# Feed-forward down projections on one core: pairs of chunks as seven block products, weight sums made by adding transfers

## The chip, the cores and the metric

The kernel runs on one NeuronCore of a Trainium2 chip. The metric is the device time of one execution in microseconds (us), as the median of several runs. Engines are named as the profile names them: PE (TensorE), DVE (VectorE), ACT (ScalarE), POOL (GpSimd), SP (SyncE, which here only issues transfers). 1 MiB is 1.0486 MB.

## What is computed

Two stacked model blocks on 256 tokens of width 1024. The first has two layers (a state-space mixer, then a neighbourhood attention), each with two feed-forward parts; these four are what the change is about, and the code numbers them 0 to 3:

```python
def swiglu(x, w_gu, w_down):                 # w_gu: 1024 x 5632, w_down: 2816 x 1024
    g, u = jnp.split(x @ w_gu, 2, axis=-1)
    return (jax.nn.silu(g) * u) @ w_down
...
h = h + 0.5 * swiglu(rmsnorm(h, ffn1_norm[i]), ffn1_w_gu[i], ffn1_w_down[i])
...
h = h + 0.5 * swiglu(rmsnorm(h, ffn2_norm[i]), ffn2_w_gu[i], ffn2_w_down[i])
gate = jax.nn.sigmoid(rmsnorm(h, ple_norm[i]) @ ple_w_gate[i])
```

The second block is an attention with three branches and a plain MLP. All is float32.

## The kernel before

**Precision.** PE multiplies in a reduced float32 form. So each operand is split into a high part and the rest (`whi` and `wlo` of a weight, `aThi` and `aTlo` of an activation), and each block product of 128 x 128 by 128 x 512 is three matmuls: high by high, high by low, low by high.

**Weight tiles.** `plan_of` (L156) lists all weight tiles in the order in which PE takes them. A tile is up to 2048 floats a partition, 1 MiB. SP's `load` (L498) brings it into one of four slots `raw`; it first waits until the split of the tile four places back is done. ACT copies it to `whi` (`ahead` in `scalar`, L1412) as soon as PE has released the tile three places back, DVE subtracts to get `wlo` (L1967), and PE's `take` waits for both. ACT, DVE and PE each run their own list in program order; `ahead` runs three tiles ahead of the work in it.

**A feed-forward part.** `ffn` goes over 11 column chunks c. A chunk takes two tiles `("up", i, c, 0)` and `(.., 1)`: 48 matmuls for both halves of the tokens. In the middle of chunk c PE turns the previous chunk's activation `fa` by four transposes (`turn_a`), ACT copies the bank to `aThi` (`high_a`) and DVE makes `aTlo` (`low_a`). At the end of a chunk ACT computes the silu and DVE the product (`fa`). Then `down` multiplies the 22 chunks of 128 rows of `w_down`: for each of the two column halves of 512, six tiles, for every 128-row chunk and each token half three matmuls, 264 in all. Banks 6 and 7 collect the left half, 2 and 3 the right one; DVE adds 0.5 times them to `h` (`residual`), and the turns of `h` for the next stage run within the right half.

**POOL** makes small statistics (`rstds`), some products of the mixer, and the bias tables `bm` of the neighbourhood attention from a table `tb`, which SP loads early in feed-forward part 2. No transfer is issued from POOL.

Of the kernel before, what the change touches and what calls it, by code (L numbers as in the profile page):

```python
# [12 lines left out]
P = 128  # L13
# [5 lines left out]
TILE = 2048  # L19

# [23 lines left out]
def constants():  # L44
# [30 lines left out]
    "a_weigh": "exps", "v_outputs": "yev yg yTlo", "a_outputs": "yThi ysq",  # L75
# [69 lines left out]
class Plan:  # L145
# [5 lines left out]
    def add(self, label, pieces, a, b):  # L151
        self.index[label] = len(self.tiles)
        self.tiles.append((pieces, a, b))


def plan_of(dr):  # L156
    p = Plan()

    def ffn(i, up, down, extra=None):
# [64 lines left out]
PREP = (8, 16, 24)  # L224
HALVES = 2 * len(PREP) + 2
# [129 lines left out]
def programs(dr, mem, banks, plan, ev):  # L355
# [11 lines left out]
    pool_tiles = set()  # L367
# [126 lines left out]
    def sync(S):  # L494
# [22 lines left out]
        def table():  # L517
            rp = dr["rpb"]
            S.wait_ge(*at("h", 4, 1, 1))
# [40 lines left out]
    def tensor(T):  # L560
# [13 lines left out]
        def take(*label):  # L574
# [5 lines left out]
            T.wait_ge(*at("w_lo_p" if n in pool_tiles else "w_lo", n))  # L580
# [115 lines left out]
        def closing_block(labels, bs, xhi, xlo, first, between=None):  # L696
# [6 lines left out]
            for t in range(2):  # L703
                for i, (label, hi, lo, kk) in enumerate(held):
                    nk = hi.shape[1]
                    for k in range(nk):
# [4 lines left out]
                        if between and t and i == 0 and k == 1:  # L711
                            between()
# [11 lines left out]
        def down(name, xhi, xlo, tiles, r, turn_last):  # L724

            for c in range(2):
                bs = ACC[c]
                clear(*bs)
                for y in range(tiles - 2):
# [3 lines left out]
                    if y == 0:  # L733
                        if c == 0:
                            turn_last()
                        elif r < 10:
                            turn(r, 0, 0)
                            turn(r, 1, 0)
                closing_block([name + (c, tiles - 2), name + (c, tiles - 1)], bs, xhi, xlo, 4 * (tiles - 2),
                              (lambda: turn(1, 0, 1)) if c and r == 1 else None)  # L740
                residual_in(r, c, bs)

        def ffn(i, r, extra=None):
# [24 lines left out]
            down(("down", i), aThi, aTlo, 6, r + 1, lambda: turn_a(10))  # L768
# [636 lines left out]
    def scalar(A):  # L1405
# [8 lines left out]
        def ahead(m):  # L1414
            while A.ready < min(m, len(plan.tiles)):
# [3 lines left out]
                if n >= NSPL:  # L1419
                    A.wait_ge(*at(*named(plan_labels[n - NSPL])))  # L1420
# [1392 lines left out]
```

## Time and profile before

| | |
|---|---|
| median of 3 runs | 1678.08 us (1678.04 to 1678.16) |
| profiled execution, span from first to last instruction | 1676.1 us |
| PE busy | 1664.8 us |
| DVE busy | 1068.0 us |
| ACT busy | 898.6 us |
| POOL busy | 86.1 us |
| DMA | 300.58 MB, 179 GB/s mean |

The page gives the profiled execution's span and no other time of its own; the median of the runs is 1.98 us longer than that span, which is what lies around the span. Busy time of PE overlaps from one matmul to the next, so a matmul's cost is read from the distance of two starts, not from its length. A DMA share is the time that packets took as a share of 16 engines; it can read above 1, because packets overlap.

### The profile page before, as it was taken

What the parts mean: (1) busy time and instruction counts of PE and PEld (TensorE: products, weight loads), DVE (VectorE), ACT (ScalarE), POOL (GpSimd) and SP (SyncE); (2) the same over time, 40 slices, a digit from 0 to 9 for tenths busy, and PEclk for the clock granted to TensorE, in tenths of its full rate; (3) what the DMA queues carried; (4) which work ended last, traced back from release to release, by engine and by line L of the source; (5) the groups of instructions that cost most, each with busy time, mean ns of one, the idle gap of its engine ahead of it and who ended that gap; (6) DMA issues with size and microseconds to landing.
All of it is one profiled execution on the core that took longest, in us unless ns stands there. A gap on an engine that the chain in (4) does not pass through costs nothing.

```text
span 1676.1 us, 23021 instructions
## 1 busy us (share of the span) xinstructions
PE 1664.8 (99%) x9366; PEld 1426.7 (85%) x9366; DVE 1068.0 (64%) x1364; ACT 898.6 (54%) x1279; POOL 86.1 (5%) x79
## 2 busy tenths in 40 slices
PE   8999999999999999999999999999999999999998
PEld 6888899999788888888888778888889999988886
DVE  5554678999965545755457766555655577766643
ACT  5443566777864444744346665444553556564532
POOL 0000000000100000000007500000000000000000
PEclk9999999999999999999999999999999999999999
DMA  9655567666466554686555336655565533465551
GB/s 306 192 178 184 158 191 208 179 196 209 156 200 198 187 188 165 188 242 209 181 175 195 119 101 214 185 180 188 180 197 153 174 103 126 152 211 178 176 192 60
DMA packets 243978, 300.58 MB, mean 179 GB/s; under 512 B 9248, under 2 KB 175520, under 8 KB 243872
## 3 DMA queue, kind: packets, MB, share of 16 engines
q1 hardware_dynamic: 238224, 289.25, 54.5%
q10 hardware_dynamic: 5648, 9.85, 2.2%
q8 instruction: 75, 1.23, 0.3%
q14 instruction: 31, 0.25, 0.0%
HBM read 297.96 MB, written 1.11 MB: 178 GB/s over the span
## 4 chain that ended last, share of the span: by engine, by line
PE 99%; DVE 1%; DMA 0%; ACT 0%; ACTq 0%; DVEq 0%; issue 0%
PE bank L564 95%; PE bank L567 4%; DMA h<-in_x 0%; DVE wlo L1967 0%; DVE hTlo L1970 0%; DVE xn L1970 0%; DVE h L1970 0%; ACT hThi L1412 0%; DVE xn L2019 0%; DVEq L2740 0%; ACT xn L1409 0%; ACTq L1924 0%; ACTq L1923 0%; ACT L1920 0%; ACTq L2740 0%
## 5 line engine op out<-in xcount | busy, mean ns | idle before, releaser
L1967 DVE TENSOR_TENSOR wlo<-raw,whi 128x2048 fp32r<-128x2048 f32 (+2 forms) x284 | 622.4, 2195 | 326.5 <-ACT whi L1412 326.5
L1412 ACT ACTIVATE whi<-raw 128x2048 fp32r<-128x2048 f32 (+2 forms) x284 | 518.2, 1832 | 244.8 <-PE bank L564 240.9
L564 PE MATMUL bank<-whi,hThi 128*128 128x512 f32 x1056 | 420.7, 398 | 0.0
L564 PE MATMUL bank<-wlo,hThi 128*128 128x512 f32 x1056 | 412.3, 390 | 0.3 <-DVE wlo L1967 0.3
L564 PE MATMUL bank<-whi,hTlo 128*128 128x512 f32 x1056 | 396.8, 391 | 0.0
L564 PE MATMUL bank<-hThi,whi 128*128 128x256 f32 x888 | 253.3, 285 | 0.0
L564 PE MATMUL bank<-hThi,wlo 128*128 128x256 f32 x888 | 251.2, 283 | 0.0
L564 PE MATMUL bank<-hTlo,whi 128*128 128x256 f32 x888 | 251.2, 283 | 0.0
L564 PEld LDWEIGHTS bank<-whi,hThi 128*128 128x128 f32 x1056 | 198.6, 188 | 44.3 <-issue 6.0
L564 PEld LDWEIGHTS bank<-whi,hTlo 128*128 128x128 f32 x1056 | 198.5, 188 | 42.6 <-DVE hTlo L1970 0.3
L564 PEld LDWEIGHTS bank<-wlo,hThi 128*128 128x128 f32 x1056 | 198.8, 188 | 40.5 <-DVE wlo L1967 1.8
L564 PEld LDWEIGHTS bank<-hThi,whi 128*128 128x128 f32 x888 | 169.5, 191 | 3.6 <-issue 3.1
L564 PEld LDWEIGHTS bank<-hThi,wlo 128*128 128x128 f32 x888 | 169.5, 191 | 0.2
L564 PEld LDWEIGHTS bank<-hTlo,whi 128*128 128x128 f32 x888 | 169.5, 191 | 0.2
L564 PE MATMUL bank<-whi,aThi 128*128 128x512 f32 x352 | 137.8, 391 | 0.0
L564 PE MATMUL bank<-whi,aTlo 128*128 128x512 f32 x352 | 137.1, 389 | 0.0
L564 PE MATMUL bank<-wlo,aThi 128*128 128x512 f32 x352 | 137.0, 389 | 0.0
L1412 ACT ACTIVATE aThi<-bank 128x512 fp32r<-128x512 f32 x44 | 26.3, 598 | 155.1 <-PE bank L567 155.1
L1409 ACT ACTIVATE ftmp<-bank,st 128x256 f32<-128x256 f32 x88 | 41.5, 475 | 105.6 <-PE bank L564 105.5
L2564 POOL TENSOR_TENSOR st<-st,cst 128x1 f32<-128x1 f32 (+2 forms) x35 | 36.5, 1057 | 1147.4 <-DVE st L1992 1075.2
L1967 DVE TENSOR_TENSOR aTlo<-bank,aThi 128x512 fp32r<-128x512 f32 x44 | 30.4, 691 | 80.8 <-ACT aThi L1412 80.8
L564 PEld LDWEIGHTS bank<-whi,aTlo 128*128 128x128 f32 x352 | 66.1, 188 | 13.8
(222 smaller groups left out, 1883.4 us busy)
## 6 DMA issues: line engine op xcount, KB each, us to landing
raw<-in_ffn_w_gu SPq DMA_DIRECT2D x172, 512.0 KB, 4.9
raw<-in_ffn_w_down SPq DMA_DIRECT2D x40, 1024.0 KB, 5.0
raw<-in_w_in SPq DMA_DIRECT2D x30, 1024.0 KB, 5.2
raw<-in_ssd_w_in SPq DMA_DIRECT2D x16, 1024.0 KB, 5.6
raw<-in_ssd_w_in SPq DMA_DIRECT2D x32, 512.0 KB, 5.5
raw<-in_w_up SPq DMA_DIRECT2D x16, 1024.0 KB, 5.4
raw<-in_w_down SPq DMA_DIRECT2D x16, 1024.0 KB, 5.0
raw<-in_na_w_qkv SPq DMA_DIRECT2D x12, 1024.0 KB, 5.2
```

What stands on the lines that cost most here:

```text
L564: return T.e.matmul(out, lhsT, rhs, start=start, stop=stop, skip_group_check=skip)
L567: return T.e.transpose(out, in_, ident)
L1409: return e.activation(out, in_, func, **kw)
L1412: return e.activation(out, in_, ACT.Identity, **kw)
L1967: return e.tensor_tensor(out, a, b, op)
L2564: return e.tensor_tensor(out, a, b, op)
```

## The change

The activations and weights of two neighbouring 128-row chunks form two by two blocks: A11, A12 for tokens 0 to 127 (first and second chunk), A21, A22 for tokens 128 to 255; B11, B12 for the first chunk's rows (left and right columns), B21, B22 for the second's. Eight block products become seven:

| bank | activation | weight | weight from |
|---|---|---|---|
| 0 | A11 | B11 | tile `paired`, 3 blocks |
| 6 | A12 | B21 | `paired` |
| 2 | A12 + A21 - A11 - A22 | B22 | `paired` |
| 4 | A21 - A22 | B11 + B12 | tile `mixed`, 4 blocks |
| 5 | A21 - A11 | B12 + B22 | `mixed` |
| 1 | A11 + A22 - A21 | B11 + B12 + B22 | `mixed` |
| 7 | A22 | B11 + B12 + B21 + B22 | `mixed` |

This is done for seven pairs (14 of the 22 chunks) in each of the four parts. The activation differences are made on POOL (`differences`), the weight sums in DRAM by transfers that POOL issues, three of four with `accum_op=ALU.add`. A "beat" `mix(b)` first waits for all transfers of the beat before and then issues up to four, each for another pair: the copy of pair b, the first addition of pair b-1, the second of b-2, the last of b-3. `BEATS` and `SSD_BEATS` say where beats stand: in part 0 at ten of eleven chunks, then eight in the mixer, four in part 1, three in part 2, six in part 3.

```diff
+PAIRS = (7, 7, 7, 7)
+MIX = [(i, j) for i in range(4) for j in range(PAIRS[i])]
+BEATS = ((1, 2, 3, 4, 5, 6, 7, 8, 9, 10), (1, 3, 5, 7), (1, 4, 7), (0, 1, 2, 3, 4, 5))
+SSD_BEATS = (1, 25, 3)
...
+                p.add(("paired", i, x), [wsrc(down, 2 * x, 2, 0, 512), wsrc(down, 2 * x + 1, 1, 512, 512)], 3, 512)
+                p.add(("mixed", i, x), [dr["mix"][i, x]], 4, 512)
...
+            if labels[n][0] == "mixed":
+                S.wait_ge(*at("m_last", *labels[n][1:]))
...
-            S.wait_ge(*at("h", 4, 1, 1))
+            S.wait_ge(*at("w_rel", "mixed", 2, PAIRS[2] - 1))
...
-            if n == tile["up", 2, 0, 0] + 8:
+            if n == tile["qkv", NA_CHUNKS[1], 0]:
                 table()
...
+            def seven(j):
+                first, final = j == 0, j == PAIRS[i] - 1
+                hi, lo = take("paired", i, j)
+                T.wait_ge(*at("aTlo", i, j))
+                T.wait_ge(*at("dTlo", i, j))
+                three_products(0, block_of(2 * j, 0), hi[:, 0, :], lo[:, 0, :], first, final)
+                three_products(2, difference(j, 2), hi[:, 2, :], lo[:, 2, :], first, False)
+                three_products(6, block_of(2 * j + 1, 0), hi[:, 1, :], lo[:, 1, :], False, False).then_inc(
+                    *sig("w_rel", "paired", i, j))
+                hi, lo = take("mixed", i, j)
...
+            def high_d(c):
+
+                A.wait_ge(*at("dsum", i, c))
+                d = mem["dsum"][:, c % 2, :]
+                copy(aThi[:, 2 * c, P:256], d[:, 0:P])
+                copy(flat(mem["dThi"][:, c, :, :]), d[:, P:512]).then_inc(*sig("dThi", i, c))
...
+                if 1 <= c <= PAIRS[i]:
+                    high_d(c - 1)
...
+            def merged():
+
+                um, wm = flat(mem["ftmp"][:, :, :]), flat(fa[:, :, :])
+                V.wait_ge(*at("root", i))
+                stt(h[:, 0, chunk(0)], banks[0], 0.5, h[:, 0, chunk(0)], ALU.mult, ALU.add).then_inc(*sig("h11", i))
...
+        def differences(i, c):
+
+            a, d = mem["araw"][:, c % 2, :], mem["dsum"][:, c % 2, :]
...
+            G.wait_ge(*at("araw", i, c))
+            if c >= 2:
+                G.wait_ge(*at("dTlo", i, c - 2))
+            tt(pairs(d[:, 0:256]), a[:, P:256].unsqueeze(1).to_broadcast([P, 2, P]), outer, ALU.subtract).then_inc(*sig("dpair", i, c))
+            G.wait_ge(*at("dpair", i, c))
+            tt(d[:, 256:384], a[:, 384:512], d[:, 0:P], ALU.subtract).then_inc(*sig("droot", i, c))
+            G.wait_ge(*at("droot", i, c))
+            tt(d[:, 384:512], a[:, 256:384], d[:, 256:384], ALU.subtract).then_inc(*sig("dsum", i, c))
...
+        def mix(b):
+
+            ready("m_copy", b - 1)
+            ready("m_first", b - 2)
+            ready("m_second", b - 3)
+            ready("m_last", b - 4)
+            if b < len(MIX):
+                i, j = MIX[b]
+                e.dma_start(dr["mix"][i, j], block(i, j, 1, 0).to_broadcast([P, 4, 512])).then_inc(*sig("m_copy", i, j, by=16))
+            if 0 <= b - 1 < len(MIX):
+                i, j = MIX[b - 1]
+                e.dma_start(dr["mix"][i, j, :, 0:3, :], block(i, j, 0, 0).to_broadcast([P, 3, 512]), accum_op=ALU.add).then_inc(*sig("m_first", i, j, by=16))
...
+        def ffn(i, extra=None):
+
+            n = tile["up", i, 0, 0]
+            for c in range(11):
+                if c < PAIRS[i]:
+                    differences(i, c)
+                if c == 2 and extra is not None:
+                    ple_rstd(extra)
+                if c in BEATS[i]:
+                    mix_at(tile["up", i, c, 0])
```

`high_d(c - 1)` stands at the end of chunk c in `scalar`, `merged` in `vector`, `differences`, `mix` and the last `ffn` on POOL. `mix_at(n)` waits for `whi` of tile n and runs the next beat. After the pairs, `merged` adds the shared banks into `h` by six DVE instructions of 128 x 512, ACT copies bank 0, and POOL adds the two right-hand sums. The eight chunks outside the pairs keep three matmuls a product; the turns of `h` for the next stage move to the last tiles.

**POOL, feed-forward part 0.** Before, POOL had these rows from the start to the middle of the attention (`st` are statistics, `gate` a product of the mixer):

```order
L2564 TENSOR_TENSOR st<-st,cst 128x1 x4
L2564 TENSOR_TENSOR gate<-gate 128x512 x6
L2564 TENSOR_TENSOR st<-st,cst 128x2
L2564 TENSOR_TENSOR st<-st,cst 128x1 x10
L2564 TENSOR_TENSOR st<-st,cst 128x8 x2
L2564 TENSOR_TENSOR bm<-tb,cst 128x256 x6
```

Now (`araw` is the turned activation, `dsum` the differences, `mix` the sums in DRAM):

```order
L2759 TENSOR_TENSOR dsum<-araw 128x256
L2759 TENSOR_TENSOR dsum<-araw,dsum 128x128 x2
L2859 DMA mix<-in_ffn_w_down 512x1x512
L2862 DMA mix<-in_ffn_w_down 128x3x512
L2865 DMA mix<-in_ffn_w_down 128x3x512
L2868 DMA mix<-in_ffn_w_down 128x512
L2759 TENSOR_TENSOR dsum<-araw 128x256
L2759 TENSOR_TENSOR dsum<-araw,dsum 128x128 x2
```

The differences of one chunk stand behind the transfers of the beat before them on the same engine.

**ACT, one chunk of feed-forward part 0.** Before:

```order
L1409 ACTIVATE ftmp<-bank,st 128x256 x2
L1412 ACTIVATE whi<-raw 128x2048
L1412 ACTIVATE aThi<-bank 128x512
L1412 ACTIVATE whi<-raw 128x2048
L1409 ACTIVATE ftmp<-bank,st 128x256 x2
L1412 ACTIVATE whi<-raw 128x2048
```

Now:

```order
L1530 ACTIVATE ftmp<-bank,st 128x256 x2
L1533 ACTIVATE aThi<-dsum 128x128
L1533 ACTIVATE dThi<-dsum 128x384
L1533 ACTIVATE whi<-raw 128x2048
L1533 ACTIVATE araw<-bank 128x512
L1533 ACTIVATE aThi<-bank 128x128
L1533 ACTIVATE aThi<-bank 128x256
L1533 ACTIVATE whi<-raw 128x2048
L1530 ACTIVATE ftmp<-bank,st 128x256 x2
```

The two copies from `dsum`, which wait for POOL, stand ahead of the split of the next weight tile.

**SP, the down projection of part 0.** Before, twelve tiles:

```order
L508 DMA raw<-in_ffn_w_gu 128x4x256 x40
L508 DMA raw<-in_ffn_w_down 128x4x512 x5
L508 DMA raw<-in_ffn_w_down 128x2x512
L508 DMA raw<-in_ffn_w_down 128x4x512 x5
L508 DMA raw<-in_ffn_w_down 128x2x512
L508 DMA raw<-in_ssd_w_in 128x8x64
```

Now (the first two of seven pairs shown):

```order
L555 DMA raw<-in_ffn_w_down 128x4x512
L547 DMA raw<-in_ffn_w_down 128x2x512
L548 DMA raw<-in_ffn_w_down 128x512
L555 DMA raw<-mix 128x2048
L555 DMA raw<-in_ffn_w_down 128x2x512
L547 DMA raw<-in_ffn_w_down 128x2x512
L548 DMA raw<-in_ffn_w_down 128x512
L555 DMA raw<-mix 128x2048
```

Each pair loads 0.75 and 1 MiB where two chunks of 1024 columns were 1 MiB, and each `raw<-mix` waits for the pair's last addition.

## Rows read from the trace of the kernel before

**Rows 1.** The page, parts 1 and 3: span, busy time, DMA queues.
```profile
span 1676.1 us, 23021 instructions
PE 1664.8 (99%) x9366; PEld 1426.7 (85%) x9366; DVE 1068.0 (64%) x1364; ACT 898.6 (54%) x1279; POOL 86.1 (5%) x79
...
q1 hardware_dynamic: 238224, 289.25, 54.5%
```
**Rows 2.** The page, part 4: the chain that ended last.
```profile
PE 99%; DVE 1%; DMA 0%; ACT 0%; ACTq 0%; DVEq 0%; issue 0%
```
**Rows 3.** Windows by stage: up 0, down 0, mixer, up 1, up 3.
```profile
core 0: us, PE busy (x) PEld busy (x) DVE busy (x) ACT busy (x) POOL busy (x), PEclk, DMA share, GB/s
36.90:136.90 100.00, 100.00 (x459) 82.74 (x458) 54.91 (x44) 44.37 (x44) 0.00 (x0) 1.00 0.58 186
136.90:198.40 61.50, 61.50 (x281) 50.98 (x280) 27.68 (x29) 24.84 (x32) 0.00 (x0) 1.00 0.57 175
198.40:480.00 281.60, 281.54 (x2166) 263.07 (x2165) 254.22 (x390) 207.33 (x361) 12.21 (x10) 1.00 0.64 187
480.00:604.60 124.60, 124.60 (x571) 103.07 (x570) 71.97 (x67) 60.80 (x66) 3.77 (x4) 1.00 0.61 194
...
1003.50:1127.40 123.90, 123.90 (x568) 102.23 (x567) 72.53 (x70) 62.37 (x71) 4.12 (x4) 1.00 0.62 195
```
**Rows 4.** Timeline of PE in down 0; 55 matmuls lie between the two.
```profile
149.65 0.39 PE L564 MATMUL bank<-whi,aThi 128*128 128x512 f32 x1
...
162.34 0.39 PE L564 MATMUL bank<-whi,aTlo 128*128 128x512 f32 x1
```
**Rows 5.** Timeline of ACT and of DVE within one chunk of up 0.
```profile
86.19 0.60 ACT L1412 ACTIVATE aThi<-bank 128x512 fp32r<-128x512 f32 x1 [3.60 <-PE bank L567]
...
80.82 0.48 DVE L1970 SCALAR_TENSOR_TENSOR fa<-bank,st,ftmp 128x256 f32<-128x256 f32 x1 [0.86 <-ACT ftmp L1409]
92.19 0.48 DVE L1970 SCALAR_TENSOR_TENSOR fa<-bank,st,ftmp 128x256 f32<-128x256 f32 x1 [0.88 <-ACT ftmp L1409]
```
**Rows 6.** Groups of down 0: the splits of weight tiles, and `h`.
```profile
L1967 DVE TENSOR_TENSOR wlo<-raw,whi 128x2048 fp32r<-128x2048 f32 x8 | 18.3, 2291 | 17.8 <-ACT whi L1412 17.8
L1412 ACT ACTIVATE whi<-raw 128x2048 fp32r<-128x2048 f32 x9 | 17.1, 1912 | 16.9 <-PE bank L564 16.9
L1967 DVE TENSOR_TENSOR wlo<-raw,whi 128x1024 fp32r<-128x1024 f32 x2 | 2.5, 1226 | 4.6 <-ACT whi L1412 4.6
L1970 DVE SCALAR_TENSOR_TENSOR h<-bank,h 128x512 f32<-128x512 f32 x3 | 2.0, 684 | 2.7 <-PE bank L564 2.7
```
**Rows 7.** Group of POOL over the span.
```profile
L2564 POOL TENSOR_TENSOR bm<-tb,cst 128x256 f32<-128x256 f32 x32 | 33.6, 1086 | 0.9 <-DVE st L2320 0.9
```
**Rows 8.** Timeline of DVE and of POOL at one place of up 1.
```profile
505.76 2.28 DVE L1967 TENSOR_TENSOR wlo<-raw,whi 128x2048 fp32r<-128x2048 f32 x1
...
505.20 0.54 POOL L2564 TENSOR_TENSOR st<-st,cst 128x1 f32<-128x1 f32 x1 [24.49 <-DVE st L2105]
505.92 2.52 POOL L2564 TENSOR_TENSOR st<-st,cst 128x1 f32<-128x1 f32 x1 [0.18 <-DVE st L2105]
```
**Rows 9.** DMA in 40 slices of 14 to 37 us: rows of 1 KB.
```profile
GB/s 355 355 354 345 347 353 346 346 349 347 354 345 347 349 326 210 127 271 349 383 383 406 340 346 360 354 349 349 331 356 353 351 351 346 340 351 315 219 358 344
```
**Rows 10.** DMA in 40 slices of 140 to 198 us: rows of 2 KB in the first half.
```profile
GB/s 0 7 201 408 107 0 140 410 174 25 314 384 181 404 150 0 0 158 408 157 0 17 304 41 169 12 82 280 344 18 19 184 362 246 302 300 111 318 297 41
```
**Rows 11.** DMA issues: KB each, median us from issue to landing.
```profile
raw<-in_ffn_w_down SPq DMA_DIRECT2D x40, 1024.0 KB, 5.0
tb<-in_rpb SPq DMA_DIRECT2D x2, 1000.0 KB, 14.6
```
**Rows 12.** DMA issues from 0 to 41.3 us.
```profile
raw<-in_ffn_w_gu SPq DMA_DIRECT2D x18, 512.0 KB, 6.9
raw<-in_ffn_w_gu SPq DMA_DIRECT2D x6, 256.0 KB, 6.4
raw<-in_ffn_w_gu SPq DMA_DIRECT2D x4, 128.0 KB, 3.9
```

More of the change, by code:

```diff
@@ L1 @@
+import itertools
 from contextlib import ExitStack
@@ L224, with down_tiles @@
 PREP = (8, 16, 24)
+BEATS = ((1, 2, 3, 4, 5, 6, 7, 8, 9, 10), (1, 3, 5, 7), (1, 4, 7), (0, 1, 2, 3, 4, 5))
+SSD_BEATS = (1, 25, 3)
+def down_tiles(pairs):
+    tiles, middle, last = {}, ([], []), [(0, 18, 22), (1, 16, 20), (1, 20, 22)]
+    for c, end in ((0, 18), (1, 16)):
+        for k in range(2 * pairs, end, 4):
+            middle[c].append((c, len(middle[c])))
+            tiles[middle[c][-1]] = (k, min(4, end - k))
+    closing = []
+    for c, k, end in last:
+        closing.append((c, sum(x[0] == c for x in tiles)))
+        tiles[closing[-1]] = (k, end - k)
+    others = [x for pair in itertools.zip_longest(middle[1], middle[0][1:]) for x in pair if x]
+    order = [("rest", middle[0][0])]
+    for j in range(pairs):
+        order.append(("pair", j))
+        if others:
+            order.append(("rest", others.pop(0)))
+    return order + [("rest", x) for x in others], tiles, closing
 HALVES = 2 * len(PREP) + 2
@@ new lines, in mixed_down @@
+            def mixed_down(r):
+                order, _, last = down_tiles(PAIRS[i])
+                take("down", i, 0, 0)
+                low_a(10)
+                for what, x in order[1:]:
+                    if what == "rest":
+                        take("down", i, *x)
+                        continue
+                    take("paired", i, x)
+                    take("mixed", i, x)
+                take("down", i, *last[0])
+                merged()
+                V.wait_ge(*at("h21", i))
+                for t in range(2):
+                    residual(r, t, 0, half(("down", i) + last[0], t), 6 + t, 0.5)
+                take("down", i, *last[1])
+                early_quarters(r)
+                V.wait_ge(*at("h22", i))
+                for t in range(2):
+                    residual(r, t, 1, half(("down", i) + last[2], t), 2 + t, 0.5)
+                    if r == 1 and t == 0:
+                        low(1, 0, 1)
+                        mean_square(1, 0)
+                if r == 1:
+                    scaled(0)
+                take("down", i, *last[2])
+                if r == 1:
+                    mean_square(1, 1)
+                    low(1, 1, 1)
+                    scaled(1)
+                else:
+                    late_quarters(r)
@@ L2637, in three @@
             for what, n in three_steps():
-                if what == "gate" and n % 2 == 0:
-                    take("gate", n // 2)
-                elif what == "keep" and n in (3, 7):
+                if what == "keep" and n in (3, 7):
                     br = n // 4
```

258 lines of the change are left out of this document (187 added, 71 removed).

## Prediction

> **What bounds the kernel now.** I read the page first. PE is busy for 99% of the span, no other engine reaches 65%, and the transfers take 54.5% of 16 engines [rows 1]. The chain of waits that ended last is PE for 99% [rows 2]: what PE does is the time, and whatever makes it wait adds to it in full. The windows by stage say so for each part: PE is busy for the whole of every feed-forward stage, at a granted clock of 1.00 (2.4 GHz), while DVE has 55 of 100 us in the up stage and 28 of 61.5 in the down stage, POOL nothing, and DMA a share of 0.57 to 0.62 [rows 3]. A matmul of 128 x 512 costs the distance of two starts: (162.34 - 149.65) / 56 = 0.2266 us [rows 4].
>
> **What is taken away.** Each pair has seven products where it had eight, three matmuls each, so 3 x 0.2266 = 0.68 us; 28 pairs give 84 matmuls and **-19.0 us**. The stationary operands change in the same rhythm as before, so I cost the others as they are.
>
> **The split of the larger tiles** runs beside PE. A pair's 21 matmuls take 4.76 us. DVE needs 2.29 us for the mixed tile and, between 1.23 and 2.29 [rows 6], 1.76 us for the paired one, 4.05 of 4.76. For the mixed tile PE's release must lead to its start within the two tiles between (also 4.76 us), and ACT 1.91 and DVE 2.29 take 4.20. Both hold with half a microsecond left. A load takes 5.0 us alone [rows 11]; four slots turn once in two pairs, 9.5 us, and 5.0 + 1.91 + 2.29 = 9.2. So nothing, at best; a load that lands 1 us late costs 0.35 us a pair or, from the second pair on, 2 us a part. I take 0 and keep 8 us for the range.
>
> **The merge.** `merged` is six DVE instructions of 0.68 us [rows 6], 4.1, plus two residuals, before PE's first turn of `h`, which stands 33 matmuls (7.5 us) behind the last mixed product: covered, at most 0.5 us a part late. **The table** `tb` is loaded after part 2, not early in it: 14.6 us [rows 11], and the weight tile queued behind it on SP is wanted 24 us after its start; covered.
>
> **POOL's differences** are three instructions a chunk: 1.09 us for 128 x 256 [rows 7] and 0.54 (128 x 1, rows 8) to 1.09 for each 128 x 128, some 2.3 us together (at 0.6 each). They start 0.6 us after ACT begins the copy at 86.19, and ACT wants them after the silu, when DVE starts `fa` at 92.19 [rows 5]: 5.4 us of room. I take 0. The trace has a reason for doubt: a POOL instruction of 128 x 1 that takes 0.54 us took 2.52 when a DVE split of a weight tile began 0.16 us before it, and both ended within 0.4 us [rows 8]. One such meeting makes 4.6 us of the 2.3, still inside 5.4; two would not be (a rival, below).
>
> **The weight sums** are the large unknown, since the trace has neither a DRAM-to-DRAM transfer nor an addition. A beat in full swing writes 1 + 0.75 + 0.75 + 0.25 = 2.75 MiB. The nearest rows are loads: when the queue is full, rows of 1 KB move at about 350 GB/s [rows 9], 3.0 us a MiB, rows of 2 KB at 400 [rows 10], 2.62 us a MiB, and mixing has rows of 2 KB. Lower bound: an addition costs what a copy costs, factor 1. Upper bound of the same rows: it must fetch both addends, so two rows are read for one written, factor 2. I take **2**, because the sixteen engines must read every byte that enters the sum, and nothing in the code spares the second read. The Trainium skill states that price (Collectives: The Full Stack, "The bandwidth ceiling"): a reduce emits two read descriptors where a copy emits one, measured at a ratio of 1.93; by it the sum below would be about 4 us smaller.
>
> Part 0. The first beat follows the turn in the chunk that holds 41.3 us (chunk 2). The mixed tile of the last pair must be split before its first product: 171 matmuls after the start of down 0, at 136.9 + 39.2 = 176.1, less 4.2 for the split, so it must have landed by 171.9. That is 130.6 us. To be moved in it:
> - ten copies, nine and eight additions of 0.75 MiB, seven of 0.25: 10 + 14.5 x 2 = 39 MiB at 2.62, 102 us;
> - up tiles: 9 + 1.5 + 0.5 = 11 of 22 MiB have been issued by then [rows 12], 11 are left, at 3.0, 33 us;
> - down tiles up to that one: 1 + 0.5 + 7 x 1.75 = 13.75 MiB at 2.62, 36 us.
> Together 171 us, **+40 us** that PE must wait. How it comes to wait: beat b waits for all transfers of beat b-1, the next chunk's differences stand behind it on POOL, ACT waits for them ahead of the split of the next weight tile, and PE for the split; in down 0 SP itself waits for the last addition, with every later tile behind it.
>
> Part 3. Six beats in its first six chunks; the differences of chunk 6 stand behind beats 25 to 29 having landed, 3 copies and 8 MiB of additions: 3 + 16 = 19 MiB, 50 us, with 13.5 MiB of loads, 40.5 us: 90.3 us. Room: 6.5 chunks of 92.19 - 80.82 = 11.37 us [rows 5] less POOL's 2.3, 71.6. **+19 us.**
>
> Part 1 has four beats in every second chunk: two have to land in 62 us, 9 MiB (24 us) and 11.5 MiB of loads (35 us): 0. Part 2 has three: 0. The mixer's eight move 36 MiB, 94 us, beside loads at 187 GB/s [rows 3] that need about half of the engines in the 207 us up to POOL's first product there: just full, 0, with up to 10 us above.
>
> Sum: -19 + 40 + 19 = +40 on the span of 1676.1, 1716; with the 1.98 us by which the median exceeds that span, **1718 us**.
>
> **Rivals.**
> - *Additions at the price of a copy.* The rows read show engines that move 400 GB/s; if an addition is limited by what it writes, part 0 needs 24.5 x 2.62 + 33 + 36 = 133 us of 130.6, +2.6, and part 3 11 x 2.62 + 40.5 = 69 of 71.6, 0. Time 1678 - 19 + 3 = **1662**, faster. Against it: both addends must be read. The sign turns at a factor of about 1.3: per unit of it part 0 grows by 14.5 x 2.62 = 38 us and part 3 by 21.
> - *The down stage runs on its loads.* With the factor at 1, pairs that take 5.1 us in place of 4.76 (a load of 6 us) and late turns take 8 to 15 us back: **1674 to 1680**, no change. For it: 1.75 MiB in 4.76 us is 385 GB/s of 400. Against: seven tiles are ahead when the stage begins.
> - *POOL is late by itself.* Two meetings with splits in a chunk make 2.3 + 4.6 = 6.9 us of 5.4: ACT waits 1.5 us in each of 28 chunks, 42 us, on top of the forecast **1760** (on top of the copy price 1704). Against it: DVE starts its second split of a chunk only after `aTlo`, so one meeting is the rule. The Trainium skill (SBUF — State Buffer, "Who interferes with whom") has this as a rule: a DVE instruction with two SBUF inputs and a GpSimd one that reads SBUF exclude each other for the whole of whichever began first. Rows 8 agree. Issuing would do the same as a meeting: 1408 rows of 2 KB a beat are told to the engines by POOL, and the trace has no row of it.
>
> **Chances.** Factor about 2: 0.47, 1718. POOL late by itself: 0.15, 1760. Copy price: 0.30, 1662. Down stage on its loads: 0.08, 1677. So slower by over 0.2% 0.62, faster by over 0.2% 0.30, within 0.2% 0.08 (0.2% is about what a measurement of this kernel can tell from no change). The range reaches from the copy price with nothing lost, 1659, to a little above the late POOL, 1768; beyond it lies factor 2 at the mean rate of the whole span, 289.25 MB in 54.5% of 1676.1 us or 317 GB/s [rows 1], near 1775. The slower cases' own range is 1700 to 1768.
>
> **What would show it.** 84 matmuls fewer. In the windows of up 0 and up 3 a DMA share near 1, PE short of the window's length, POOL waiting for transfers, ACT's `dThi<-dsum` and `aThi<-dsum` waiting for POOL; up 0 longer than 124 us, down 0 over 56. In down 1 and down 2 about 56 us in place of 61. I am wrong if an addition lands in about the time of a copy of its size, if the DMA share in up 0 stays under 0.9, or if POOL ends its differences within 5 us of ACT's `araw` in every chunk.

## The result, and the profile after

| | before | after |
|---|---|---|
| median | 1678.12 us (1678.04 to 1679.06) | 1899.54 us (1893.66 to 1903.79) |
| span of the profiled execution | 1676.1 us | 1898.7 us |
| PE busy | 1664.8 us | 1700.7 us |
| POOL busy | 86.1 us | 264.0 us |
| DMA | 300.58 MB | 403.38 MB |

The ratio is 1.1315, 95% interval 1.1294 to 1.1336: 13% slower. The forecast was 1718 us, and the upper end of its range 1768. The sign was right and the size was not: a loss of 221 us where 40 were forecast. Every ratio below is taken against runs of the kernel before from the same session; the ratio of f_four leaves out one of its six runs, which took 2959.35 us at a mean granted clock of 0.554, for a reason that is not known.

The page of the changed kernel, parts 1, 3 and 4; its rows answer to [rows 1] and [rows 2]:

```profile
span 1898.7 us, 23570 instructions
PE 1700.7 (90%) x9282; PEld 1445.0 (76%) x9282; DVE 1147.6 (60%) x1500; ACT 969.5 (51%) x1423; POOL 264.0 (14%) x283
...
q1 hardware_dynamic: 239120, 311.28, 51.1%
q0 software_dynamic: 34048, 80.75, 22.5%
...
PE 56%; DMA 28%; SPq 5%; ACT 4%; DVE 4%; POOL 2%; issue 1%; ACTq 0%; DVEq 0%; POOLq 0%
```

PE has 9282 matmuls where it had 9366: the 84 matmuls are gone. But PE no longer sets the end. It was 99% of the chain, now it is 56%, and 28% are transfers. Queue q0 is new: it holds the weight sums. PE's busy time rose by 36 us, although 84 matmuls, 19 us, are gone: in the windows below TensorE's granted clock is lower in the stages where PE waits.

The windows by stage answer to [rows 3]. They are cut at the first and the last matmul of each down projection: up 0, down 0, mixer (two rows, the second with up 1), down 1, up 2, down 2, attention with up 3, down 3, and the rest.

```profile
core 0: us, PE busy (x) PEld busy (x) DVE busy (x) ACT busy (x) POOL busy (x), PEclk, DMA share, GB/s
0.00:156.70 156.70, 137.12 (x592) 111.02 (x593) 79.83 (x101) 73.80 (x114) 31.67 (x45) 0.95 1.00 265
156.70:296.70 140.00, 69.41 (x259) 53.43 (x259) 44.42 (x42) 36.46 (x40) 19.66 (x18) 0.76 0.89 221
296.70:530.00 233.30, 184.69 (x1392) 179.94 (x1391) 145.06 (x230) 112.08 (x171) 34.57 (x34) 0.88 0.96 222
530.00:781.20 251.20, 242.25 (x1346) 203.62 (x1345) 182.89 (x246) 160.28 (x281) 44.97 (x48) 0.98 0.80 226
781.20:843.90 62.70, 58.10 (x256) 46.04 (x255) 46.12 (x39) 37.67 (x36) 2.99 (x2) 1.00 0.91 312
843.90:1002.40 158.50, 152.50 (x690) 125.14 (x689) 94.29 (x116) 85.71 (x128) 26.36 (x37) 0.98 0.82 222
1002.40:1063.20 60.80, 58.38 (x255) 47.46 (x254) 44.42 (x37) 35.88 (x34) 3.00 (x2) 0.97 0.88 277
1063.20:1350.00 286.80, 259.11 (x1226) 205.06 (x1225) 167.44 (x278) 149.71 (x255) 86.72 (x85) 0.95 0.72 195
1350.00:1411.10 61.10, 58.41 (x256) 47.43 (x255) 44.41 (x37) 35.91 (x34) 3.01 (x2) 0.97 0.83 295
```

The same cuts in every kernel that was run (us; "rest" is 487.5 to 487.8 in all of them and left out):

| | up 0 | down 0 | mixer, up 1 | down 1 | up 2 | down 2 | attention, up 3 | down 3 |
|---|---|---|---|---|---|---|---|---|
| before | 136.9 | 61.5 | 406.2 | 61.0 | 149.8 | 61.0 | 250.9 | 61.0 |
| after | 156.7 | 140.0 | 484.5 | 62.7 | 158.5 | 60.8 | 286.8 | 61.1 |
| e1_no_sums | 137.8 | 61.8 | 406.2 | 60.8 | 149.9 | 60.5 | 250.9 | 61.6 |
| e2_plain_copies | 137.6 | 113.0 | 444.6 | 59.9 | 149.8 | 60.5 | 256.3 | 61.2 |
| e3_beats_only | 151.6 | 65.8 | 515.5 | 61.0 | 168.4 | 61.0 | 269.6 | 61.0 |
| g_part0 | 153.1 | 141.4 | 406.2 | 60.8 | 149.8 | 60.8 | 250.9 | 60.8 |
| e_half | 136.4 | 57.6 | 406.2 | 56.7 | 149.8 | 56.6 | 251.0 | 56.8 |
| f_four | 137.0 | 59.7 | 406.2 | 58.8 | 149.9 | 58.8 | 251.0 | 58.8 |
| f_five | 137.2 | 61.4 | 406.2 | 60.4 | 149.8 | 60.4 | 251.1 | 60.4 |
| f_five_pool | 136.6 | 72.3 | 406.5 | 69.9 | 149.8 | 71.6 | 250.9 | 72.8 |

So the 222.6 us of span are: part 0 +98.3 (up 0 +19.8, down 0 +78.5), mixer with up 1 +78.3, up 2 +8.7, attention with up 3 +35.9, and the other three down stages +1.6 together, where -14.3 were forecast. Beyond the +40 that were forecast, the largest piece is the mixer's 78, then part 0's (98 against 40 less 5 of products), then part 3's.

**Part 0 is a chain of beats.** The chain of waits of the changed kernel, 221 to 270 us:

```profile
221.30 0.78 POOL mix L2859
222.07 1.28 POOL mix L2862
223.36 0.22 POOL mix L2865
223.58 19.95 DMA mix<-in_ffn_w_down
...
244.13 0.77 POOL mix L2859
...
246.32 21.49 DMA mix<-in_ffn_w_down
...
267.88 4.72 DMA raw<-mix
```

The last transfer of a beat is issued 2.3 us after the first, it lands 20 us later, and only then does the next beat start. The ten beats of part 0 start from 44.1 to 244.1 us, 22.2 us apart on the mean (the first three are short, since they have one, two and three transfers; the full ones are 22.8 to 27.9 apart, 25.0 on the mean). The last one has landed just before SP loads the last mixed tile, at 267.88: 44.1 + 9 x 22.2 + 23.7. In down 0 ACT waits 70.2 us, in six places, for a mixed tile, and in the whole stage PE works 69.41 of 140 us, at a mean granted clock of 0.76 where it was 1.00 (2.4 GHz) [rows 3].

The DMA queues from 44.1 to 267.9 us, which is the chain from its first beat to the last landing:

```profile
q0 software_dynamic: 10528, 25.69, 60.5%
q1 hardware_dynamic: 16810, 25.51, 35.0%
```

These are the bytes of the prediction's sum (24.5 MiB of copies and additions, 24.75 MiB of loads, 25.69 and 25.95 MB). But by these shares they held the sixteen engines for 135 and 78 us of the 223.8, where 102 and 69 were priced. By the shares the engines stood empty for some 10 us only. Since packets overlap, a share can read some per cent high (108% in one row below), so this is a split to a few microseconds.

**In up 0 the chain reaches PE through POOL.** Timeline of POOL, then of ACT, at the longest stall:

```profile
120.16 0.78 POOL L2859 DMA_DIRECT2D mix<-in_ffn_w_down  x1 [20.01 <-DMA mix<-in_ffn_w_down]
...
122.97 2.13 POOL L2759 TENSOR_TENSOR dsum<-araw 128x256 f32<-128x256 f32 x1
125.19 0.99 POOL L2759 TENSOR_TENSOR dsum<-araw,dsum 128x128 f32<-128x128 f32 x2
```
```profile
126.21 0.31 ACT L1533 ACTIVATE aThi<-dsum 128x128 fp32r<-128x128 f32 x1 [20.05 <-POOL dsum L2759]
```

POOL waited 20 us for the beat before it could issue the next one and make the differences; ACT waited 20 us for the differences, with the next weight tile's copy behind it.

**In the mixer the loads get too little.** DMA by queue, 370 to 376 us, inside a beat:

```profile
q0 software_dynamic: 474, 0.92, 87.2%
q1 hardware_dynamic: 491, 0.25, 20.5%
```

While additions are under way the two queues move about the same number of packets, here 474 and 491 in 6 us, but a packet of q0 is 2 KB and one of these loads 512 bytes. q1 so got 0.25 MB in 6 us, 42 GB/s, where the mixer uses 187 [rows 3]. The chain of waits in the mixer runs through loads that take 22 to 28 us from issue to landing, two of them:

```profile
330.44 28.11 DMA raw<-in_ssd_w_in
...
380.03 24.02 DMA raw<-in_ssd_w_in
```

The weight sums' queue from 296.7 to 530 us held the engines for half of the stretch, 119 us:

```profile
q0 software_dynamic: 9728, 23.07, 50.9%
```

Over the program the median landing of these loads went from 5.6 us (1 MiB) and 5.5 us (512 KB) to what part 6 of the page shows:

```profile
raw<-in_ssd_w_in SPq DMA_DIRECT2D x16, 1024.0 KB, 21.6
raw<-in_ssd_w_in SPq DMA_DIRECT2D x32, 512.0 KB, 17.1
```

The Trainium skill (DMA: Bandwidth & Descriptors, "Queues, rings and completion order") states that each DMA engine serves the queue rows that have work in turn and changes rows only between packets; by a packet it means a batch of some 9 to 17 descriptors, not one row as the profile counts them. The equal counts agree with turns of equal numbers of rows; how many rows make a turn no run here shows.

Of the 78 us of the mixer and up 1, about 21 are matmuls that ran slower: PE is busy for 184.69 + 242.25 = 426.9 us, where it was for 406.1, at granted clocks of 0.88 and 0.98 in place of 1.00. The other 57 us PE stands still.

### The profile page after: what moved, and what is told of

It is laid out like the page before. It is cut to its first block, busy times and chain, and to the rows that moved or that the text cites. A ratio compares the mean times of both kernels' runs of the same rounds, so it can differ in the third digit from the quotient of the medians.

```text
span 1898.7 us, 23570 instructions
## 1 busy us (share of the span) xinstructions
PE 1700.7 (90%) x9282; PEld 1445.0 (76%) x9282; DVE 1147.6 (60%) x1500; ACT 969.5 (51%) x1423; POOL 264.0 (14%) x283
## 2 busy tenths in 40 slices
DMA packets 278927, 403.38 MB, mean 212 GB/s; under 512 B 11937, under 2 KB 178209, under 8 KB 275233
## 4 chain that ended last, share of the span: by engine, by line
PE 56%; DMA 28%; SPq 5%; ACT 4%; DVE 4%; POOL 2%; issue 1%; ACTq 0%; DVEq 0%; POOLq 0%
PE bank L610 53%; DMA mix<-in_ffn_w_down 12%; DMA raw<-in_ssd_w_in 6%; DMA raw<-in_ffn_w_gu 5%; SPq L555 4%; DMA raw<-mix 4%; ACT whi L1533 3%; DVE wlo L2118 3%; PE bank L613 3%; DMA raw<-in_na_w_qkv 1%; POOL mix L2862 1%; POOL mix L2859 0%; DMA raw<-in_ffn_w_down 0%; POOL dsum L2759 0%; DMA h<-in_x 0%
## 5 line engine op out<-in xcount | busy, mean ns | idle before, releaser
L2118 DVE TENSOR_TENSOR wlo<-raw,whi 128x2048 fp32r<-128x2048 f32 (+3 forms) x312 | 670.7, 2156 | 460.2 <-ACT whi L1533 460.0
L1533 ACT ACTIVATE whi<-raw 128x2048 fp32r<-128x2048 f32 (+3 forms) x312 | 560.8, 1803 | 445.0 <-PE bank L610 158.1
L610 PE MATMUL bank<-hThi,whi 128*128 128x256 f32 x888 | 262.1, 295 | 54.9 <-issue 54.9
L610 PEld LDWEIGHTS bank<-whi,hTlo 128*128 128x128 f32 x1056 | 201.7, 191 | 44.1 <-DVE hTlo L2121 0.3
L610 PEld LDWEIGHTS bank<-hThi,wlo 128*128 128x128 f32 x888 | 177.4, 200 | 0.2
L610 PE MATMUL bank<-whi,dThi 128*128 128x512 f32 x84 | 37.2, 442 | 76.8 <-DVE wlo L2118 74.1
L610 PE MATMUL bank<-whi,aThi 128*128 128x512 f32 x240 | 97.6, 407 | 2.8 <-issue 2.7
L610 PE MATMUL bank<-wlo,aThi 128*128 128x512 f32 x240 | 95.9, 400 | 0.0
L610 PE MATMUL bank<-whi,aTlo 128*128 128x512 f32 x240 | 95.8, 399 | 0.0
L610 PEld LDWEIGHTS bank<-whi,dThi 128*128 128x128 f32 x84 | 17.1, 204 | 86.4 <-issue 71.1
L2859 POOL DMA_DIRECT2D mix<-in_ffn_w_down x28 | 22.0, 785 | 360.6 <-DMA mix<-in_ffn_w_down 220.1
## 6 DMA issues: line engine op xcount, KB each, us to landing
mix<-in_ffn_w_down POOLq DMA_DIRECT2D x56, 768.0 KB, 17.6
```

The lines of the kernel that those rows point to most:

```text
L610: return T.e.matmul(out, lhsT, rhs, start=start, stop=stop, skip_group_check=skip)
L1533: return e.activation(out, in_, ACT.Identity, **kw)
L2118: return e.tensor_tensor(out, a, b, op)
L2859: e.dma_start(dr["mix"][i, j], block(i, j, 1, 0).to_broadcast([P, 4, 512])).then_inc(*sig("m_copy", i, j, by=16))
```

## The experiments

**e1_no_sums.** The change without any sum: the mixed tile is loaded from other rows, nothing waits for it.

```diff
-                p.add(("mixed", i, x), [dr["mix"][i, x]], 4, 512)
+                p.add(("mixed", i, x), [up[0:P, 0:2048].rearrange("p (k c) -> p k c", k=4)], 4, 512)
...
-            if labels[n][0] == "mixed":
-                S.wait_ge(*at("m_last", *labels[n][1:]))
...
-            G.wait_ge(*at("w_hi", n))
-            mix(next(beats))
+            return
```

> The changed kernel without any transfer that makes weight sums; the mixed tiles (same size, rows of 8 KB) are loaded from another weight and nothing waits for a sum, so the output is not the reference's. Theory A (all of the loss comes from the sums, and in the down stages the loads of 1.75 MiB a pair take back the 19 us of products): 1674 to 1684 us, each down stage 60 to 61 us. Theory B (the products' saving is real, the down stages were only disturbed by sums): 1657 to 1664 us, each down stage about 56 us.

Measured: 1679.75 us, ratio 1.0007 (0.9998 to 1.0016). All of the 221 us come with the sums. POOL's differences are all still there: each of the 28 of 128 x 256 takes 0.74 us, and no engine waits for one. But the 19 us of products are not there either: each down stage lasts 60.5 to 61.8 us, with 21 matmuls fewer. Window of down 1:

```profile
605.80:666.60 60.80, 58.43 (x256) 47.44 (x255) 44.42 (x37) 35.99 (x34) 3.00 (x2) 0.97 0.86 293
```

DMA share 0.86 where it was 0.57 [rows 3, down 0]. PE stands still for 2.4 us, and its granted clock is 0.97.

**e_half.** e1_no_sums with a quarter of each mixed tile loaded; the splits are as large as before. The edit against e1_no_sums:

```diff
+            if labels[n][0] == "mixed":
+                e.dma_start(slot[:, 0:1, :], pieces[0][:, 0:1, :]).then_inc(*sig(f"d_w{n % NRAW}", n, by=16))
+                return
```

> As e1_no_sums, but a mixed tile loads one of its four blocks (256 KB in place of 1 MiB); the other three hold what was in the slot, so the four parts' results are not the reference's. Theory A (in e1 the down stage ran on its loads: 1.75 MiB in a pair of 4.76 us): with 1 MiB a pair each down stage takes about 56.3 us in place of 60.5 to 61.8, total 1657 to 1664 us. Rival B (the stage runs on the chain release, ACT's copy, DVE's split, with 4.05 of 4.76 us of DVE work): the split is as large as before, so the stages stay at 60 to 62 us and the total at 1676 to 1680. Between them: both bind, 1666 to 1674.

Measured: 1663.24 us, ratio 0.9911 (0.9898 to 0.9924). Theory A held. Window of down 1:

```profile
600.20:656.90 56.70, 56.70 (x256) 46.45 (x255) 44.50 (x37) 35.98 (x34) 3.00 (x2) 1.00 0.70 233
```

DVE and ACT do the same work as in e1_no_sums (44.50 and 35.98 us against 44.42 and 35.99), PE never waits, and the stage is 4.1 us shorter: the 2.4 us of standing still are gone, and 1.7 us more come from a clock of 1.00 in place of 0.97. The two loads of a paired tile land after 3.9 and 4.1 us (medians) where they took 5.6 and 5.8 in e1_no_sums. So the down stages of e1_no_sums lose the products to the size of the loads, and so, with loads of the same sizes, do down 1 to 3 of the changed kernel, where PE works 58.1 to 58.4 of 60.8 to 62.7 us.

**e2_plain_copies.** The change with the same transfers, but none of them adds; the mixed weights are copies of one block, not sums.

```diff
-                e.dma_start(dr["mix"][i, j, :, 0:3, :], block(i, j, 0, 0).to_broadcast([P, 3, 512]), accum_op=ALU.add)
+                e.dma_start(dr["mix"][i, j, :, 0:3, :], block(i, j, 0, 0).to_broadcast([P, 3, 512]))
```

(and the other two alike)

> The changed kernel with the three adding transfers of each pair as plain copies to the same places, so the sums are not sums. Theory A (an added 2 KB row holds an engine for about 176 ns where a copied one takes 84, and loads get one packet for each of them): beats of 12 to 15 us in place of 23, total 1700 to 1770 us. Rival C (the cost lies in POOL's queue itself: issue, start, landing, and waiting for the beat before): beats of 20 us or more, total 1850 us or more.

Measured: 1777.74 us (1772.41 to 1785.22), ratio 1.0607 (1.0583 to 1.0631). Neither theory's range: the adding itself costs 122 of the 221 us, the beats 98 even as plain copies, 51 of it in down 0. Full beats start 17.3 to 22.1 us apart in part 0, 19.6 on the mean, against 25.0 with additions: of the beats, rival C was nearly right, theory A (12 to 15 us) was not. A landing of the 768 KB transfers fell only from 17.6 to 14.7 us (medians over the program). The same 24.5 MiB, all of it copied now, held the engines for 50.1% of the 176.8 us from 43.2 to 220, that is 3.6 us a MiB where the prediction had 2.62:

```profile
q0 software_dynamic: 6800, 25.66, 50.1%
```

The cheap rival of the prediction, 1662 us, would have been wrong even with the addition at the price of a copy.

**e3_beats_only.** The kernel before, with the 31 beats added on POOL; nothing waits for them but the next beat. The results are unchanged.

```diff
+            for c in range(11):
+                if c in BEATS[i]:
+                    mix_at(tile["up", i, c, 0])
...
+        for k in range(*SSD_BEATS):
+            mix_at(tile[SSD_TILES[k]])
```

> The kernel before with the 31 beats of transfers added at the same places and nothing that uses or waits for them but the next beat; the products are the old ones and the output is whole. Theory A (the loads are starved beside adding transfers, most where their rows are short, in the mixer): 1740 to 1800 us, of it 60 us or more in the mixer, 0 to 15 in each up stage. Rival B (the loss is the chain of waits POOL to ACT to PE and SP's wait for the last addition): 1678 to 1695 us.

Measured: 1844.70 us (1840.31 to 1850.10), ratio 1.0993 (1.0970 to 1.1015), above the range expected: theory A's kind of loss, and more of it (up 2 alone grows by 18.6 us, where 0 to 15 were given); rival B is out. Down 0 grows by 4.3 us only, so the other 74 us there in the changed kernel are SP's and PE's wait for the sums. The mixer with up 1 grows by 109, more than in the changed kernel, because beats that down 0 does not wait for are still running there: the tenth beat of part 0 starts at 223.65 us, and down 0 ends at 217.4. Its waits, 217 to 733 us:

```profile
ACT whi L1416 <- DMA raw<-in_ssd_w_in: 101.9, 15, 18.0
```

**g_part0.** Seven pairs in part 0, one in each other part: ten beats in part 0, none in the mixer.

```diff
-PAIRS = (7, 7, 7, 7)
+PAIRS = (7, 1, 1, 1)
...
-BEATS = ((1, 2, 3, 4, 5, 6, 7, 8, 9, 10), (1, 3, 5, 7), (1, 4, 7), (0, 1, 2, 3, 4, 5))
-SSD_BEATS = (1, 25, 3)
+BEATS = ((1, 2, 3, 4, 5, 6, 7, 8, 9, 10), (4,), (4,), (4,))
+SSD_BEATS = (0, 0, 1)
```

> The change with seven pairs in part 0 and one in each other part: ten beats in part 0 as before, none in the mixer, one each in parts 1 to 3. Theory A (part 0's beats and waits by themselves cost +98 us there, the mixer's eight beats +78 there): up 0 about 157 us, down 0 about 140, mixer and up 1 406 to 412, total 1770 to 1785 us. Rival B (a part of the mixer's excess was work left over from part 0): mixer and up 1 420 us or more, total 1790 or more. Rival C (down 0's excess came from transfers for later parts): down 0 under 120 us.

Measured: 1772.63 us, ratio 1.0560 (1.0546 to 1.0574). Theory A: part 0 keeps +96 us, the mixer with up 1 is back at 406.2, so its +78 is the eight beats' own. And the last three beats, one in each of parts 1 to 3, cost nothing: 406.2, 149.8 and 250.9 us are those of the kernel before. They are small ones, with three, two and one of the four transfers, 1.75, 1 and 0.25 MiB; a full beat by itself was not tried.

**m1_transfers.** Transfers alone, one after the other and in beats, then beats beside streams of loads.

> Transfers alone, no engine computes and the output is not the reference's. First single ones, each after the one before has landed: copy of 1 MiB, copy of 0.75, additions of 0.75, 0.25 and 1 MiB (8 KB rows). Then three beats of four transfers with nothing else, then SP streaming 16 tiles of 1 MiB in rows of 512 B, 1 KB, 2 KB and 8 KB beside three beats each. Theory A: an addition takes 2 to 2.6 times the transfer time of a copy of its size over a fixed start of about 3.5 us: copy of 1 MiB 6 to 7 us, addition of 0.75 MiB 8 to 9, against about 5.5 for the copy; beats alone 18 to 20 us; loads beside additions at about 45 GB/s (512 B), 85 (1 KB), 130 (2 KB), over 250 (8 KB). Rival C: additions land within 1 us of copies, and loads keep over half of their rate whatever the row.

Measured. A copy of 1 MiB lands 7.1 us after its issue, a copy of 0.75 MiB after 6.2, an addition of 0.75 MiB after 8.5. That is theory A; rival C had the addition within 1 us of the copy. Three beats with nothing beside them, timeline of POOL (their first transfers):

```profile
99.22 0.70 POOL L3048 DMA_DIRECT2D mix<-in_ffn_w_down  x1 [34.34 <-DMA mix<-in_ffn_w_down]
...
117.95 0.77 POOL L3048 DMA_DIRECT2D mix<-in_ffn_w_down  x1 [14.57 <-DMA mix<-in_ffn_w_down]
...
136.87 0.77 POOL L3048 DMA_DIRECT2D mix<-in_ffn_w_down  x1 [14.77 <-DMA mix<-in_ffn_w_down]
```

18.8 us from beat to beat on an idle DMA system. GB/s in 40 slices, and the queue, of the first of them, 99 to 118 us:

```profile
GB/s 0 0 0 95 233 345 354 138 86 164 164 259 207 229 147 194 203 207 207 211 207 207 203 207 207 190 121 164 78 108 151 168 172 164 125 82 52 26 0 0
...
q0 software_dynamic: 1216, 2.88, 82.8%
```

82.8% of 19 us are 15.7 us in which packets held the sixteen engines, and 3 us at both ends together stand empty. Those 15.7 us are more than the bytes at the prediction's price, 4.5 x 2.62 = 11.8. The plateau of 207 GB/s is that price (two times 2.62 us a MiB would be 200 GB/s); the slices behind it fall to 78 to 190 GB/s before they run out, with packets still holding the engines. A copy has no better price when nothing waits between copies. Nine of 1 MiB in a row, 58 to 99 us, held the engines for 37.6 us, 4.2 us a MiB:

```profile
q0 software_dynamic: 2448, 9.44, 91.8%
```

Beside streams of loads, with the counts of 5 us in the middle of a beat (packets of q0 and of q1), the loads' rate in the same 5 us, and their rate with nothing beside them:

| rows of the loads | beat to beat, us | packets q0, q1 | loads, GB/s | alone, GB/s |
|---|---|---|---|---|
| 512 bytes (265 to 270 us) | 23.1, 23.7 | 404, 400 | 40 | 347 |
| 1 KB (370 to 375) | 23.9, 24.4 | 392, 394 | 78 | 386 |
| 2 KB (463 to 468) | 26.6, 27.4 | 309, 311 | 124 | 408 |
| 8 KB (553 to 558) | 41.6, 26.9 | 188, 188 | 258 | 427 |

The counts are equal in all four, so the longer row gets the larger share: theory A's 45, 85, 130 and over 250 GB/s, and not rival C's half of the rate. And beside longer rows the beats come later. The loads of 512-byte rows landed after:

```profile
raw<-in_ssd_w_in SPq DMA_DIRECT2D x10, 512.0 KB, 19.8
```

The factor of an addition against a load with rows of the same length is about 2: at their best the additions write 207 GB/s and the loads bring 408. From the counts of a queue it is 1.9: 474 packets at 87.2% of 16 engines for 6 us are 177 ns for each 2 KB that is added, in the mixer of the changed kernel; in this run's stream of 2 KB loads beside beats (453.8 to 507.8 us) a loaded packet took 57.6% x 16 x 54 us / 5409 = 92 ns:

```profile
q1 hardware_dynamic: 5409, 10.76, 57.6%
```

The Trainium skill (Collectives: The Full Stack, "The bandwidth ceiling") states a measured ratio of 1.93 between a copy and a reduce, which has two source reads; 1.9 agrees.

**f_four, f_five.** If loads and sums by transfer are the loss, the products can still be had: DVE makes the sums from the blocks that are in SBUF. Block B12 alone is loaded for a mixed tile (1 MiB a pair in place of 1.75), and with four pairs a part every pair stands beside an ordinary tile.

```diff
-PAIRS = (7, 7, 7, 7)
+PAIRS = (4, 4, 4, 4)
...
+        def block_sums(n):
+            p, m = wview("raw", n), wview("raw", n + 1)
+            V.wait_ge(*at(f"d_w{n % NRAW}", n))
+            V.wait_ge(*at(f"d_w{(n + 1) % NRAW}", n + 1))
+            tt(m[:, 0:4:3, :], m[:, 1:2, :].to_broadcast([P, 2, 512]), p[:, 0:3:2, :], ALU.add).then_inc(*sig("bouter", n + 1))
+            V.wait_ge(*at("bouter", n + 1))
+            tt(m[:, 1, :], m[:, 0, :], p[:, 2, :], ALU.add).then_inc(*sig("bthree", n + 1))
+            V.wait_ge(*at("bthree", n + 1))
+            tt(m[:, 2, :], m[:, 1, :], p[:, 1, :], ALU.add).then_inc(*sig("bsum", n + 1))
```

> Four pairs a part in place of seven, and no transfer adds anything: DVE makes the weight sums in the raw slot (block B12 is loaded, three additions of 1024, 512 and 512 elements a partition, about 2.6 us a pair by the split's price), POOL only makes the activation differences. Every pair then stands beside a tile of 24 matmuls. Theory A (products are saved, the sums by transfers and the crowded loads were the whole loss): 16 pairs x 0.68 = 10.9 us saved, total 1665 to 1670 us, down stages about 58.3 us. Rival B (DVE's or ACT's work in the down stage, or the differences, bind whatever the loads do): 1674 to 1690.

Measured: 1669.72 us, ratio 0.9950 (0.9937 to 0.9963), so 8.4 us faster than before; the five runs of the ratio lie between 1668.79 and 1672.19. The down stages are 58.8 us where 58.3 were expected (down 0: 59.7), and PE is busy for nearly the whole of them, here in down 1:

```profile
602.90:661.70 58.80, 58.68 (x265) 48.06 (x264) 47.24 (x45) 31.41 (x31) 3.00 (x2) 1.00 0.65 214
```

> As f_four with five pairs a part: 20 x 0.68 = 13.6 us saved, total 1662 to 1668 us, if DVE keeps up; the last two pairs of a part stand side by side and need 6.7 us of DVE work in 4.76 us, so 1 to 2 us a part may go: then 1666 to 1672. If DVE binds the whole stage (rival B): 1676 or more.

Measured: 1676.51 us, ratio 0.9991 (0.9982 to 0.9999): rival B's time. Down 1 to 3 take 60.4 us, 2.8 more than the products allow (61.0 less five times 0.68). The chain of waits in down 1:

```profile
632.88 1.11 issue
633.99 1.23 DVE raw L2121
...
635.24 0.70 DVE raw L2121
...
635.97 0.70 DVE raw L2121
...
636.74 1.93 ACT whi L1534
```

ACT's copy of the mixed tile has to wait for all three additions. Groups of DVE there (615 to 655 us):

```profile
L2121 DVE TENSOR_TENSOR wlo<-raw,whi 128x2048 fp32r<-128x2048 f32 x8 | 18.2, 2290 | 3.5 <-ACT whi L1534 3.5
L2121 DVE TENSOR_TENSOR wlo<-raw,whi 128x1536 fp32r<-128x1536 f32 x4 | 7.0, 1751 | 0.0
L2121 DVE TENSOR_TENSOR raw<-raw 128x512 f32<-128x512 f32 x8 | 5.5, 692 | 0.3
L2121 DVE TENSOR_TENSOR raw<-raw 128x1024 f32<-128x1024 f32 x4 | 4.9, 1217 | 0.0
```

A pair needs 1.22 + 2 x 0.69 + 1.75 + 2.29 = 6.6 us of DVE for 4.76 us of PE; where two pairs and a short tile stand together, DVE's sums get into the chain. Theory A knew the 6.7 us and gave them too little.

**f_five_pool.** f_five with the last two additions on POOL.

```diff
+                if labels[n - NRAW][0] == "paired":
+                    S.wait_ge(*at("bsum", n - NRAW + 1))
...
+            for j in range(PAIRS[i]):
+                n = tile["paired", i, j]
+                p, m = wview("raw", n), wview("raw", n + 1)
+                G.wait_ge(*at("bouter", n + 1))
+                tt(m[:, 1, :], m[:, 0, :], p[:, 2, :], ALU.add).then_inc(*sig("bthree", n + 1))
+                G.wait_ge(*at("bthree", n + 1))
+                tt(m[:, 2, :], m[:, 1, :], p[:, 1, :], ALU.add).then_inc(*sig("bsum", n + 1))
```

The first two lines make SP wait for POOL before it loads over a paired tile.

> As f_five, but of the three additions that make a mixed tile DVE keeps the first (1.22 us) and POOL makes the other two (128 x 512 each, an estimate of 2.1 us each from 1.08 us for 128 x 256). Theory A (f_five lost its products because DVE had 6.65 us of work for a pair of 4.76 us; with 5.3 us it nearly keeps up): down stages 57.5 to 58.5 us, total 1662 to 1668 us. Rival B (POOL's 4.2 us stand in the chain before ACT's copy of the mixed tile, and grow where they meet DVE's splits, so that the chain is longer than with DVE): down stages over 61 us, total 1677 to 1695.

Measured: 1722.70 us, ratio 1.0261 (1.0247 to 1.0275). Rival B, and more than it gave. Groups of POOL, then waits, 604 to 680 us:

```profile
L2772 POOL TENSOR_TENSOR raw<-raw 128x512 f32<-128x512 f32 x10 | 20.1, 2010 | 87.9 <-DVE raw L2123 87.5
```
```profile
ACT whi L1536 <- POOL raw L2772: 18.5, 4, 6.8
```

4.0 us of POOL per pair stand ahead of ACT's copy, which so waits 18.5 us in a stage. Here, relieving the busy engine by a slower one within the same chain was a loss.

## Why the prediction was wrong

- **The products, -19.0 us.** The step is right: in e_half, where neither sums nor loads stand in the way, the stages are 56.6 to 56.8 us (57.6 in down 0). That is -3.9 to -4.4 a part against -4.8, and -16.8 in all.
- **"The split of the larger tiles ... So nothing, at best".** Wrong, by 4 to 5 us a part: the mechanism of the rival "the down stage runs on its loads" was at work in these stages. It had a chance of 0.08. The doubt in the prediction ("a load that lands 1 us late costs 0.35 us a pair or, from the second pair on, 2 us a part") was of the right kind. The landing of 5.0 us came from a kernel whose down stage has a DMA share of 0.57. In down 1 of the changed kernel, at 0.91, a mixed tile lands after 7.4 us.
- **The price of an addition, factor 2.** The factor is right, 1.9 to 2.0, and e2 shows what it is worth, 122 us. What it multiplies is not. 2.62 us a MiB is the best rate of loads, and e2's copies took 3.6 us a MiB in the same place, m1's row of nine 4.2.
- **"Together 171 us, +40 us that PE must wait".** This is the step that failed. The chain took 44.1 to 267.8 us, 224 and not 171; the mixed tile that was to land by 171.9 landed at 272.6, 101 us late, and part 0 grew by 98. Its bytes were right and their price was not: the beats' transfers held the engines for 135 us where 102 were summed, the loads for 78 where 69 were. By these shares, 43 us of the error of 53 are a price too low and 10 are engines with nothing to do. The empty stretches come from what the sum left out: beat b waits for all of beat b-1. Alone, a full beat takes 18.8 us, priced at 11.8; 3.1 of the 7.0 us between are empty ends, 3.9 are packets that hold the engines longer than priced. How much of those 3.9 would go if beats did not wait for each other, and more additions were under way at the end of each, no run shows.
- **Mixer, "just full, 0, with up to 10 us above".** This is the same step again, and the largest miss, 68 us beyond the 10: the eight beats' transfers held the engines for 119 us where 94 were summed, and the sum compared total work with total time. While additions are under way the loads of 512-byte rows come away with 40 to 42 GB/s, and four slots of `raw` did not bridge landings of 17 to 28 us. A mean share of 0.64 [rows 3] says nothing of a stretch of 20 us in which the share is 1.
- **Part 3, +19 us.** Measured +35.9 with the attention, by the same error. From the first of its beats, at 1206.8 us, to the landing of the fifth, at 1317.1, are 110 us, where 90 were summed and 71.6 were there. Part 1's share can't be told from the mixer's. Part 2: 8.7 us for three beats, forecast 0.
- **POOL late by itself, 1760 us.** Not the cause: with the same differences and no beats, in e1_no_sums, nothing waits for POOL. The meeting with a split that [rows 8] gave reason to fear happened twice to the 84 instructions (2.35 us at 731.2, where a split had begun at 730.7, and once at 1237.7). The 2.1 us at 96.95 and at 122.97 are of another kind: DVE is idle there, and the difference ends 0.75 us after the record of the beat's last issue, which is what it takes alone. That is the prediction's own remark that issuing would act like a meeting, and it costs 1.4 us a time. The 72 us that ACT waited for `dsum`, in seven places, belong to the beats ahead of it.
- **The merge, the table:** nothing to be seen of them; the stage after each down projection is not longer in e1_no_sums.

Of the signs named for right and wrong, those for "slower" all came (DMA share 1.00 in up 0, PE 137.12 of 156.7 us, ACT waiting for `dsum`). The one for down 1 and down 2, "about 56 us in place of 61", did not.

What stays open: how much of the 78 us of mixer and up 1 is the turns of the queues alone and how much the engines' work; no run gave the loads longer rows there. Why copies and additions hold the engines longer than loads of the same bytes, and the three microseconds at a beat's ends, were measured, not explained. No run issued beats that do not wait for each other.

## What to carry to other kernels

Where a chain of transfers waits for itself, count its links and the time from issue to last landing of each, and compare that with the time it has; the sum of bytes over the engines' best rate is only a lower bound. Take the price of a transfer from one of its own kind, in the company that it will have: a load's rate was 1.4 to 1.6 times too good for a copy within DRAM. A mean DMA share of 0.6 is no room for a second queue of large packets beside loads of short rows: look at the load's landing within the stretch of the burst, and at how many tiles stand ahead of it. A saving of products that makes each PE microsecond need 1.75 times the weights is paid at the loads; with the sums made from blocks that are in SBUF, and spread so that the splitting engine keeps up, the same idea gave 8 us here with sixteen pairs and nothing with twenty.

## What was not expected of the hardware

- An addition by transfer held its engine for 177 ns for each 2 KB, a load for 92 ns, and four transfers issued within 2.5 us, 2.75 MiB written, take 18.8 us from beat to beat with nothing beside them.
- Two queues that both have work pass the same number of packets while additions are under way, whatever the loads' rows are: 404 and 400, 392 and 394, 309 and 311, 188 and 188 in 5 us, with 512 bytes, 1, 2 and 8 KB.
- Issuing an addition shows as 1.3 to 1.9 us of POOL (means of 28: 1.34 for the first, 1.88 for the last), four transfers of a beat overlapping within 4.2 us; an instruction of POOL right behind them took 2.1 us in place of 0.74.
- A short stall costs more than itself: in down 1 of e1_no_sums 2.4 us of standing still came with 1.7 us of slower matmuls, at a granted clock of 0.97 in place of 1.00.
